# A new base address for the on-chip arena: 96 bytes higher

## The reference, cut to what matters

```
h = x + 0.5 * swiglu_ffn(rmsnorm(x))                   # ffn0
h = h + concat(short_conv, gated_deltanet) @ w_mix_out # mix
h = h + 0.5 * swiglu_ffn(rmsnorm(h))                   # ffn1
h = h + concat(gla_mixer, mem_attention) @ w_out[0]    # gla
h = h + conv_ffn(rmsnorm(h))                           # ffn2
h = h + concat(nsa_mixer, mem_attention) @ w_out[1]    # nsa
h = h + conv_ffn(rmsnorm(h))                           # ffn3
out = rmsnorm(h)
```

## The kernel before

| tensor | first byte | remainder by 256 | remainder by 64 |
|---|---|---|---|
| hT, xH, xL, raw, wH, wL, par | 16,512 and on | 128 | 0 |
| ident, ones | 100,512 and 101,024 | 160 | 32 |
| ones64, lvl | 101,568 and 102,080 | 192 | 0 |
| col, sq, rstd | 105,696, 106,208 and 110,304 | 224 | 32 |
| gate_up, b2 | 112,544 and 114,080 | 160 | 32 |
| arena (and g_hi, g_lo, w_hi3, w_lo3, m_hi, m_lo) | 114,560 | 128 | 0 |

## Time and profile before

### The profile page before, as it was taken

How to read it: one execution, slowest core, us unless ns; L and a number is a source line. 1 busy time by engine, 2 the same in 40 slices (tenths; PEclk the granted TensorE clock), 3 DMA queues, 4 the chain that set the end, 5 groups by cost and what they waited for, 6 DMA issues and landing times.

```text
span 2447.4 us, 31719 instructions
## 1 busy us (share of the span) xinstructions
PE 2382.7 (97%) x12027; PEld 1945.7 (80%) x12027; DVE 1335.6 (55%) x2053; ACT 962.2 (39%) x1464; POOL 157.1 (6%) x151
## 2 busy tenths in 40 slices
PE   8999999999999999999899999999999989999999
PEld 7888886678778888877887788888887657888887
DVE  4434337677454344346776766643535874666633
ACT  5222226634442223254334433433324873433423
POOL 3000001024020000030000100000110001000001
PEclk9999999999999999999999999999999999999999
DMA  5333322220223332332123233232744102333322
GB/s 151 94 94 99 98 87 78 77 62 17 69 86 95 94 99 91 102 96 61 44 61 95 78 95 98 90 101 89 176 130 117 47 16 78 95 94 97 100 95 78
DMA packets 319649, 215.79 MB, mean 88 GB/s; under 512 B 49305, under 2 KB 302764, under 8 KB 319544
## 3 DMA queue, kind: packets, MB, share of 16 engines
q1 hardware_dynamic: 316280, 200.40, 28.5%
q0 software_dynamic: 3264, 13.94, 1.7%
HBM read 212.17 MB, written 8.44 MB: 90 GB/s over the span
## 4 chain that ended last, share of the span: by engine, by line
PE 85%; DVE 9%; ACT 4%; issue 2%; DMA 0%; POOL 0%; POOLq 0%; DVEq 0%; ACTq 0%; SPq 0%
PE bank L589 16%; PE bank L591 16%; PE bank L590 16%; PE bank L776 6%; PE bank L777 6%; PE bank L778 6%; PE bank L956 1%; DVE arena L2740 1%; ACT wH L407 1%; DVE wL L445 1%; PE bank L2688 1%; PE bank L2225 1%; DVE xL L850 1%; DVE arena L2779 1%; PE bank L1694 1%
## 5 line engine op out<-in xcount | busy, mean ns | idle before, releaser
L589 PE MATMUL bank<-xH,wH 128*128 128x512 f32 x1920 | 763.7, 398 | 8.4 <-DVE xL L850 5.2
L591 PE MATMUL bank<-xH,wL 128*128 128x512 f32 x1920 | 751.3, 391 | 0.0
L590 PE MATMUL bank<-xL,wH 128*128 128x512 f32 x1920 | 750.9, 391 | 0.0
L445 DVE TENSOR_TENSOR wL<-raw,wH 128x1024 fp32r<-128x1024 f32 (+1 forms) x357 | 445.7, 1248 | 508.3 <-ACT wH L407 507.5
L407 ACT ACTIVATE wH<-raw 128x1024 fp32r<-128x1024 f32 (+1 forms) x357 | 374.6, 1050 | 729.4 <-PE bank L591 327.8
L589 PEld LDWEIGHTS bank<-xH,wH 128*128 128x128 f32 x1920 | 361.0, 188 | 99.4 <-issue 19.5
L590 PEld LDWEIGHTS bank<-xL,wH 128*128 128x128 f32 x1920 | 361.6, 188 | 79.1 <-issue 4.3
L591 PEld LDWEIGHTS bank<-xH,wL 128*128 128x128 f32 x1920 | 361.1, 188 | 78.3 <-issue 0.8
L776 PE MATMUL bank<-g_hi,wH 128*128 128x512 f32 x704 | 274.2, 390 | 1.5 <-DVE wL L445 1.5
L777 PE MATMUL bank<-g_lo,wH 128*128 128x512 f32 x704 | 273.9, 389 | 0.0
L778 PE MATMUL bank<-g_hi,wL 128*128 128x512 f32 x704 | 273.9, 389 | 0.0
(11 more groups left out here) (359 smaller groups left out, 2703.8 us busy)
## 6 DMA issues: line engine op xcount, KB each, us to landing
raw<-in_ffn_w_in SPq DMA_DIRECT2D x88, 512.0 KB, 3.8
raw<-in_w_up SPq DMA_DIRECT2D x88, 512.0 KB, 3.8
raw<-in_ffn_w_out SPq DMA_DIRECT2D x44, 512.0 KB, 3.4
raw<-in_w_down SPq DMA_DIRECT2D x44, 512.0 KB, 3.4
raw<-in_w_mix_in SPq DMA_DIRECT2D x28, 512.0 KB, 3.9
raw<-in_w_kv_shared SPq DMA_DIRECT2D x12, 512.0 KB, 5.2
rel_wide<-rel_rows POOLq DMA_DIRECT2D x12, 512.0 KB, 11.4
arena<-rel_wide POOLq DMA_DIRECT2D x12, 448.0 KB, 4.3
```

Source lines behind the costliest of these rows:

```text
L445: nc.vector.tensor_tensor(lo[:, 0:n], raw[:, k, 0:n], hi[:, 0:n].bitcast(F32), ALU.subtract)\
L589: pe.matmul(o, wh, xa, start=a, stop=False)
L590: pe.matmul(o, wh, xb, start=False, stop=False)
L591: last = pe.matmul(o, wl, xa, start=False, stop=z)
```

## The change

Only the formula for the arena's base changes:

```
-        at_arena = (nc.sbuf_usable_end - 4 * 14 * R - P) // 256 * 256 + P
+        at_arena = (nc.sbuf_usable_end - 4 * 14 * R) // 32 * 32
```

## The result

The changed kernel takes 2465.57 us (median of 4 runs, 2461.48 to 2468.14), the kernel before 2448.76 (4 runs, 2446.71 to 2450.32). The ratio is 1.0064, with a 95% interval of 1.005 to 1.008: slower, and above the forecast's range. The profiled execution took 2460.24 us itself, 11.1 more than the one before. The instructions are the same 31,719.

A forecast was written before the change was run, and what follows sets the result against it. The prediction took an almost gapless matmul train on TensorE to bound the kernel. Zero terms for TensorE, VectorE, ScalarE and transfers left 2449.18 us at 2449.2 us, with a whole range of 2446 to 2460.

The forecast's parts named there:

- What bounds the kernel: Whole kernel: an almost gapless train of matmuls, TensorE busy 97% of the span and 85% of the chain.
- TensorE, streamed operand: Matmuls that may read the arena: 0 change, upper bound 1.3 ns on each of 6315, 8.2 us.
- The twins: Matmuls compared at old and new phase: line 902, 592 and 592 ns; 16 transposes, 1.97 against 1.95 us.
- That is a whole number of 16 and 32 byte pieces: Arena shift of 96 bytes: phase within such pieces stays, so only what sees 64 bytes or more can change.
- VectorE, ScalarE, transfers at 0: Work outside the matmuls: 0 each; bounds +2.6 us VectorE, -2.5 us ScalarE, +2.5 us exposed transfers.
- The 5.2 us of the first load: Load of `x` at the start: staying at 5.2 us was a sign that the forecast is right.
- The transfers' rival: Exposed first load and last store: half-written 64-byte lines cost double, giving 2457.4 us; chance 0.05.
- the rule weighed there: Transfers: descriptors starting off a 256 byte boundary pay for unused bytes; 2.3% of the 3.0 us store, 0.07 us.
- slower through TensorE: Down stages: fp32r streams starting at 32 by 64 need one more access; up to 30 us, 2479 us; chance 0.09.
- the half of 14: Down stages: the fixed 14 ns of each matmul grows by half of that, giving 2464 us.
- faster through separated phases: Down stages: equal-phase streams disturb each other, so separating them saves at most 30 us, 2419 us; chance 0.07.
- Shift of the clock: Attention: one more or one fewer stretch at 1.2 GHz moves the time by a microsecond or two, inside the range.

The follow-up runs named there:

- the trains: Separate kernels computing nothing of the reference: back-to-back fp32r matmuls, streamed tile and weights at chosen addresses; 226.9 ns per matmul for 128 by 128, 233.5 for 224 by 128.
- g_back_at_128: Changed kernel with only `g_hi` and `g_lo` put back at remainder 128, arena still at 224; 2450.14 us, ratio 0.9995 to the kernel before.
- all_at_224: Changed kernel with all shared tensors moved up 96 bytes too, so streamed tiles and weights all have remainder 224; 2450.87 us, ratio 1.0002 to the kernel before.
- weights_at_160: Kernel before with the arena left at 128, raw weights, `wH`, `wL` and all behind them moved up 32 bytes; 2499.02 us, ratio 1.0197.
- own: Separate train of 48 fp32r matmuls alternating two phases; each stream matches its own weights, the next weights have the other phase; 234.0 ns per matmul.
- crossed: Separate train of 48 fp32r matmuls alternating two phases; each stream differs from its own weights but matches the next ones; 229.8 ns per matmul.

## Why the prediction was wrong

*What bounds the kernel.* Right: a train of matmuls with almost no gap, in which each ns of a matmul in the down stages counts 2112 times.

*"TensorE, streamed operand ... I take 0".* This is the step that failed. The term was 0 with an upper bound of 8.2 us; it measured 13.9 us by the trains and 13.8 at equal clock. The twins could not show it. Line 902 is plain fp32, and plain fp32 does not see the distance even in a train (429 and 429 ns from record to record). The transposes stream 128 columns, and at 128 or 256 columns the trains differ by 1 ns or nothing. The loss begins between 256 and 384 columns of fp32r (174 against 177 ns at 384), and it is large at 512 alone (6.6 ns, against 1.3 at 496). And both twins were read as "old phase, new phase" of one operand, when it is a relation of two. The bound was wrong for the same reason: 1.3 ns came from the row that is blind to the effect. The text named the gap ("what I can't read off is an fp32r matmul whose streamed tile sits at the new phase"), but put it at 0.09 and kept it out of the range.

*"That is a whole number of 16 and 32 byte pieces, so ... only what sees pieces of 64 bytes or more can change."* Right as far as it goes: distance 96 is slow, and what counts has a period of 256 bytes (distances 0 and 256 both 226.9).

*VectorE, ScalarE, transfers at 0.* Right: 684 and 632 ns and 3.0 us after as before, and g_back_at_128 shows it at the level of the whole kernel. The 5.2 us of the first load, named as a sign, read 8.61 in the chain, because the chain took the other half of `x`. One reading on the way was wrong: a row of the arena does not end "as far off" a 256 byte boundary as before; its ends went from 128 bytes off to 32. The transfers' rival is out by the same run. As for the rule weighed there (the Trainium skill, "DMA: Bandwidth & Descriptors"), a part of 0.07 us is too small for the store's 3.0 us, with one digit after the point, to confirm or refute.

*The rival "slower through TensorE".* Right in place, in count and in the sign that would show it (line 776 moves, 589 does not), and the size lay between its point of decision of 2.3 ns and the half of 14 that it priced; 2465.57 is within 1.6 us of its 2464. That nearness is luck, since no row stood behind the half. Its reason was wrong: not the start at 32 by 64 costs, for all_at_224 has just that start and loses nothing.

*The rival "faster through separated phases".* Its mirror image is what happens. It supposed that streams of equal remainder disturb each other; in fact the kernel before was fast because the two remainders were equal, and separating them costs.

*Shift of the clock.* It moved the profiled execution by about -3.5 us, more than the "microsecond or two" allowed, and the second profile of the changed kernel by +2.4.

What is shown: the distance by 256 bytes decides (trains, weights_at_160, all_at_224), and it is not, or not mainly, the distance to a matmul's own weights but to those of its neighbours (own, 234.0 ns; crossed, 229.8). That it is the load of the next weights during the stream is argued from where that load stands in the profile. That two streams of reads meet in the same part of SBUF is argued too, and against the simplest form of it speak the 3 ns left in crossed, the small difference at 96, 64 and 32 columns of weights, and the fast distances of 28 or 60 bytes. Why up to 256 columns nothing is lost stays open too. At 128 columns a matmul takes 110.6 ns, nearly as long as the 119.9 at 256, so there something other than the streamed columns sets the length and may hide the loss; at 256 no such reason can be read off.

## What to carry to other kernels

When a kernel is a train of fp32r matmuls, look at the address of the streamed tile minus that of the weights, modulo 256 bytes; keep it at 0, or at 64 if it must be another multiple of 32, and check it again when a buffer ahead of either changes size. To judge a change of address from a trace, a twin must have the same data type, the same number of columns, the same place in a train and the same partner; an isolated or shorter instruction said nothing here. And where such a twin is missing, the bound can't be taken from the nearest blind row: the unexplained part of each instruction (here 14 ns) times the count, 30 us, would have been a more honest end of the range, though nothing shows it to be a bound.

## What the runs showed of the hardware

- An fp32r matmul of 512 columns in a train takes 226.8 ns at distance 0, 229.1 at 64, and 233.2 to 234.2 at every other multiple of 32 bytes. A bf16 one takes 216 at distance 0 and 96 alike, each of the two records of a plain fp32 one 429. The 227 ns of this kernel are therefore 11 ns above what the same train does in bf16.
- The Trainium skill, "TensorE: Matmul & The Clock Gate", in "Step-by-step: what each phase is for", in its step on loading weights, says that TensorE has two independent read ports to SBUF, so that loading the next weights takes nothing from the running matmul. The bf16 trains are in line with it (216 ns at both distances, with loads of 98 ns); the fp32r ones are not: own, at 234.0, loses 7 ns by nothing but the addresses of its neighbours' weights. The same page gives the gap between matmuls of 512 columns as about 216 ns, which is the bf16 number here and not the fp32r one.
- Fewer columns of weights do not make an fp32r train faster: at distance 0 it took 226.7 ns with 128, 230.0 with 96, 230.4 with 64 and 231.3 with 32, while the load's record went from 188 ns to 161, 134 and 109.
